# A two-layer decoder step on one core: both feed-forward up projections as one level of Strassen's scheme, with their results passing through DRAM

## The reference

```
def rmsnorm(x, g):
    xf = x.astype(jnp.float32)
    y = xf * lax.rsqrt(jnp.mean(xf * xf, axis=-1, keepdims=True) + EPS)
    return (y * g.astype(jnp.float32)).astype(x.dtype)

def sq_relu_mlp(x, w_up, w_down):
    h = jax.nn.relu(x @ w_up)
    return (h * h) @ w_down
...
        h = h + mix.astype(h.dtype)
        h = h + sq_relu_mlp(rmsnorm(h, p["norm_mlp"][layer]), p["w_up"][layer], p["w_down"][layer])
```

## Time and profile before

| | us |
|---|---|
| median of 3 runs | 2968.97 |
| lowest and highest of the runs | 2967.33, 2970.69 |
| span of the profiled execution | 2965.2 |
| PE busy in it | 2851.3 (96%) |
| DVE, ACT, POOL busy | 1339.4, 517.6, 721.5 |

### The profile page before, as it was taken

One profiled execution on the slowest core, in us unless ns is written; L12 is line 12 of the kernel. 1 busy time (PEld: TensorE's weight loads), 2 busy tenths in 40 slices (PEclk: granted clock), 3 DMA queues, 4 the chain that ended last, 5 costly groups with the idle time before them and its releaser, 6 DMA issues. The chain is left out here.

```text
span 2965.2 us, 51232 instructions
## 1 busy us (share of the span) xinstructions
PE 2851.3 (96%) x21758; PEld 2709.3 (91%) x21758; DVE 1339.4 (45%) x1746; ACT 517.6 (17%) x827; POOL 721.5 (24%) x437
## 2 busy tenths in 40 slices
PE   6999999999999999999998999899999999999997
PEld 6989898889999999999988898766899999999997
DVE  6665555646422332323546666355454223332233
ACT  3222222212000000000213444333210000000001
POOL 2100000013333333333321110112233333333331
PEclk8999999999999999999999999999999999999998
DMA  4111111211111111111211001466111111111111
GB/s 110 52 53 53 53 53 53 93 33 50 44 49 45 43 50 44 43 50 43 55 38 28 30 28 34 178 262 246 41 44 43 44 50 43 49 45 43 47 47 72
DMA packets 211773, 183.92 MB, mean 62 GB/s; under 512 B 21777, under 2 KB 199745, under 8 KB 209505
## 3 DMA queue, kind: packets, MB, share of 16 engines
q1 hardware_dynamic: 176192, 123.58, 13.8%
...
## 5 line engine op out<-in xcount | busy, mean ns | idle before, releaser
L156 POOL CAST w_hi<-w_raw 128x1024 fp32r<-128x1024 f32 (+2 forms) x148 | 143.0, 967 | 1194.7 <-PEq L1227 975.7
L158 POOL TENSOR_TENSOR w_lo<-w_raw,w_hi 128x1024 fp32r<-128x1024 f32 (+2 forms) x148 | 396.7, 2681 | 11.9
L1425 DVE TENSOR_TENSOR h<-h,G 128x1050 f32<-128x1050 f32 x120 | 149.7, 1247 | 482.6 <-PE G L217 482.6
L217 PE MATMUL G<-a_lo,w_hi 128*128 128x350 f32 x1536 | 330.8, 323 | 0.0
L217 PE MATMUL G<-a_hi,w_hi 128*128 128x350 f32 x1536 | 330.6, 323 | 0.0
L217 PE MATMUL G<-a_hi,w_lo 128*128 128x350 f32 x1536 | 330.2, 323 | 0.0
L1356 ACT ACTIVATE a_hi<-ua 128x1050 fp32r<-128x1050 f32 x64 | 69.4, 1084 | 1219.9 <-DVE ua L1415 1219.9
L217 PEld LDWEIGHTS G<-a_lo,w_hi 128*128 128x128 f32 x1536 | 262.7, 189 | 0.0
L1412 DVE TENSOR_TENSOR ua<-G,rstd 128x1050 f32<-128x1050 f32 x64 | 80.1, 1252 | 402.3 <-PE G L217 402.2
L217 PEld LDWEIGHTS G<-a_hi,w_hi 128*128 128x128 f32 x1536 | 261.5, 189 | 0.0
L217 PEld LDWEIGHTS G<-a_hi,w_lo 128*128 128x128 f32 x1536 | 260.9, 189 | 0.0
...
## 6 DMA issues: line engine op xcount, KB each, us to landing
w_raw<-in_w_up SPq DMA_DIRECT2D x64, 512.0 KB, 4.2
w_raw<-in_w_down SPq DMA_DIRECT2D x64, 512.0 KB, 3.4
w_raw<-in_hg_wq SPq DMA_DIRECT2D x8, 512.0 KB, 3.8
w_raw<-in_hg_wf SPq DMA_DIRECT2D x8, 512.0 KB, 3.8
w_raw<-in_hg_wi SPq DMA_DIRECT2D x8, 512.0 KB, 3.9
w_raw<-in_hg_wg SPq DMA_DIRECT2D x8, 512.0 KB, 4.2
s_old<-in_state_hgrn ACTq DMA_DIRECT2D x8, 512.0 KB, 5.5
out_state_hgrn_sample<-s_new ACTq DMA_DIRECT2D x8, 512.0 KB, 3.7
```

What stands on the lines that cost most here:

```text
L156: nc.gpsimd.tensor_copy(high, raw).then_inc(k.w_hi_done, 1)
L158: nc.gpsimd.tensor_tensor(low, raw, high, ALU.subtract).then_inc(k.w_split, 1)
L217: last = nc.tensor.matmul(out, w(a, t), x(b, t, c), start=(t == 0 and (a, b) == ORDER[0]), stop=(t == nk - 1 and (a, b) == ORDER[-1]))
L1425: nc.vector.tensor_tensor(h, h, tile(k, (g0 + 1 + t) % 2), ALU.add).then_inc(k.g_free, 1)
```

## The change

Per layer, the up projection W^T X is cut into 2 x 2 quarters. W^T (4096 hidden features x 1024) is cut along the model's features into those of even and of odd tiles of h, and along the hidden features into even and odd blocks of 128; the 1048 tokens are cut into two halves of 524. A pair p (of 16) is two blocks of hidden features, with weight quarters A11, A12, A21, A22 of 128 x 512 numbers; the activations' quarters B11, B21, B22 and their sums T1 to T4 are made once. Per pair PE makes 7 products of half the depth and half the tokens in place of 8: a product is 4 x 3 x 2 = 24 matmuls of 262 columns. These are Strassen's scheme in the form with 15 additions: DVE makes four sums of weights S1 to S4 per pair, ACT all seven high parts, POOL all seven low parts, and the sums of products are mostly made by accumulation in PSUM, with a copy of an intermediate state (E1, E2, E3 by ACT) before the accumulation goes on, which DVE adds later. Each quarter of the result, 128 x 524, gets relu and `rstd` by DVE (`scale`), the square by ACT, and is stored to DRAM (`kept_a`).

The up projection of all hidden features now comes first, then the down projection in 8 groups, whose activations are loaded again from DRAM and split into high (ACT) and low parts (DVE). While the up projection runs, 7 of the 8 tiles of h are in DRAM (`kept_h`), and odd pairs' weights use their room. The down projection's matmuls, weight loads and splits are as before. Semaphores of the recurrent layer are given back so that there are enough for `Mlp`.

```diff
-W_GROUP, G_GROUP = 8, 12
+W_GROUP, G_GROUP = 4, 8
+HALF = PROMPT // 2 + DEC // 2
+QUARTER = HALF // 2
+PAIRS = D_FF // (2 * P)
+KH = KD // 2
...
+OPERANDS = {"P1": ("A11", "B11"), "P2": ("A12", "B21"), "P3": ("S4", "B22"), "P4": ("A22", "T4"),
+            "P5": ("S1", "T1"), "P6": ("S2", "T2"), "P7": ("S3", "T3")}
+WEIGHTS = ("A11", "A12", "S2", "S1", "S3", "A22", "S4")
...
     def pool(self, pool):
+        for p in range(PAIRS):
+            for x in WEIGHTS:
+                pool.wait_ge(self.w_high, self.at("w_high", WEIGHT[x, p]))
+                pool.wait_ge(self.summed, self.at("summed", SUM["S3" if x == "A11" else "S4", p]))
+                nc.gpsimd.tensor_tensor(self.w_lo[p % 2][x][:, :, :], self.w_raw[p % 2][x][:, :, :],
+                                        self.w_hi[p % 2][x][:, :, :], ALU.subtract).then_inc(self.w_ready, 1)
         split_blocks(k, pool, W_GROUP * GROUPS, n0=self.w0)
...
+        def product(x, p, slot, first=False):
+            a, b = OPERANDS[x]
+            pe.wait_ge(self.w_ready, self.at("w_ready", WEIGHT[a, p]))
...
+            for j in range(KH):
+                if p == 0:
+                    pe.wait_ge(self.x_low, self.at("x_low", LOW_X[b, j]))
+                for u, v in ORDER:
+                    for c in range(2):
+                        last = nc.tensor.matmul(self.bank(slot, c), w[u][:, j, :],
+                                                moving[v][:, j, c * QUARTER:(c + 1) * QUARTER],
...
+        product("P1", 0, "a0", True)
+        product("P2", 0, "b", True)
+        pe.wait_ge(k.g_free, g0)
+        norm()
+        for i in range(PAIRS):
+            if i > 0:
...
+                product("P1", i, f"a{i % 2}", True)
+                pe.wait_ge(self.early_out, self.at("early_out", EARLY_OUT["E3", i - 1]))
+                product("P4", i - 1, f"a{(i - 1) % 2}")
+                pe.wait_ge(self.taken, self.at("taken", TAKEN["C11", i - 1]))
+                product("P2", i, "b", True)
+                pe.wait_ge(self.taken, self.at("taken", TAKEN["C22", i - 1]))
+                product("P3", i - 1, "c")
+            pe.wait_ge(self.early_out, self.at("early_out", EARLY_OUT["E1", i]))
+            product("P6", i, f"a{i % 2}")
+            if i > 0:
+                pe.wait_ge(self.taken, self.at("taken", TAKEN["C12", i - 1]))
...
+            product("P5", i, "c", True)
+            pe.wait_ge(self.early_out, self.at("early_out", EARLY_OUT["E2", i]))
+            product("P7", i, f"a{i % 2}")
...
+        dve.wait_ge(self.squared, self.at("squared", QUARTERS["C12", last]))
+        for j in range(RINGS):
+            dve.wait_ge(self.a_stored[j], self.at("a_stored", 16 * (4 * PAIRS // RINGS)))
+        clear(1)
+        clear(2)
+        for t in range(KD):
+            if t < KD - 1:
+                dve.wait_ge(self.h_back[t], self.at("h_back", 16))
+            add(g0, t)
```

More of the change, by code:

```diff
@@ new lines, with counted, in_steps @@
+SUMS = ("S1", "S2", "S3", "S4")
+FIRST_X, LATER_X = ("B11", "B21", "T2", "T1"), ("T3", "T4", "B22")
+LAST_WEIGHT_AT = ("A11", "A12", "S2", "S1", "S3", "A22", "S4")
+def counted(*events):
+    return {e: n + 1 for n, e in enumerate(events)}
+def in_steps(early, late, middle=(), last=()):
+    out = []
+    for i in range(PAIRS + 1):
+        out += [(e, i - 1) for e in early if i > 0]
+        out += [(e, i) for e in middle if i < PAIRS]
+        out += [(e, i - 1) for e in late if i > 0]
+        out += [(e, i) for e in last if i < PAIRS]
+    return out
@@ new lines, in product_order @@
+def product_order():
+    out = []
+    for i in range(PAIRS + 1):
+        for e, lag in (("P1", 0), ("P4", 1), ("P2", 0), ("P3", 1), ("P6", 0), ("P5", 0), ("P7", 0)):
+            if 0 <= i - lag < PAIRS:
+                out.append((e, i - lag))
+    return out
+PRODUCT = counted(*product_order())
+EARLY_OUT = counted(*in_steps(("E3",), (), ("E1",), ("E2",)))
+QUARTERS = counted(*in_steps(("C22", "C21"), ("C12",), ("C11",)))
+TAKEN = counted(*[e for e in QUARTERS if e[0] != "C21"])
+WEIGHT = counted(*[(x, p) for p in range(PAIRS) for x in WEIGHTS])
@@ new lines, in norm @@
+        def norm():
+            pe.wait_ge(self.sq_summed, self.at("sq_summed", SQUARE[KD - 1, 1]))
+            for n in range(4):
+                last = nc.tensor.matmul(self.bank("a1" if n >= 2 else "c", n % 2), k.ones[:, :],
+                                        k.rstd[:, n * QUARTER:(n + 1) * QUARTER], start=True, stop=True)
+            last.then_inc(self.norm_done, 1)
+        pe.wait_ge(k.g_free, g0 - 1)
+        for b in range(2):
+            pe.wait_ge(k.m_free[b], k.m_read[b])
@@ new lines, in pe @@
+        pe.wait_ge(k.w_split, w0 + 3)
+        pe.wait_ge(self.quarter, self.at("quarter", QUARTERS["C21", last]))
+        for n, col in enumerate((0, P)):
+            if n:
+                pe.wait_ge(self.taken, self.at("taken", TAKEN["C12", last]))
+            for t in range(GROUP):
+                if n == 0:
+                    pe.wait_ge(self.a_ready, self.at("a_ready", t + 1))
+                ins = products(nc, banks(k, (g0 + n) % 2), w_parts(k, 0, 2 * P, col), moving(0), (t,), GROUP)
+            ins.then_inc(k.g_done, 1)
@@ L1394, in pe @@
[L1394 removed]
+                group(i * 2 + 1 + half, 1 + half)
+        group(GROUPS - 1, 1)
         if self.latent_next:
@@ new lines, in dve @@
+        dve.wait_ge(k.dve_apart, self.layer + 1)
+        for j in range(KH):
+            dve.wait_ge(self.x_exact, self.at("x_exact", EXACT_X["T4a", j]))
+            raw = self.op_raw["T4"][:, j, :]
+            nc.vector.scalar_tensor_tensor(out=raw, in0=self.side(2 * j, 0), scalar=k.g_back[:, 2 * j:2 * j + 1],
+                                           in1=raw, op0=ALU.mult, op1=ALU.add).then_inc(self.x_exact, 1)
+        for j in range(KH):
+            self.low_x(dve, "T3", j)
+        dve.wait_ge(self.rooted, self.at("rooted", 2))
@@ new lines, in dve, with add, group @@
+        last = PAIRS - 1
+        clear(0)
+        for j in range(GROUP):
+            low_a(0, j, 0)
+        take("C22", last)
+        take("C21", last)
+        take("C12", last)
+        def add(g, t):
+            dve.wait_ge(k.g_done, g + t + 1)
+            h = in3(k.h[:, t, :])
+            nc.vector.tensor_tensor(h, h, tile(k, (g0 + t) % 2), ALU.add).then_inc(k.g_free, 1)
+        def group(g, buffer):
+            for t in range(KH):
+                add(g_at(g), t)
+            for j in range(GROUP):
+                low_a(g + 1, j, buffer)
+            for t in range(KH, KD):
+                add(g_at(g), t)
@@ L1444, in dve @@
         else:
-            take_down(g_last)
+            for t in range(KD):
+                add(g_last, t)
 class Keys:
```

613 lines of the change are left out of this document (481 added, 132 removed).

## The result

The changed kernel takes 2922.4 us (median of 4 runs, 2921.6 to 2924.6) against 2969.5 for the kernel before: a ratio of 0.9848, 95% interval 0.9834 to 0.9862, faster by 47 us. Measured again beside later experiments it was 2921.5 against 2967.0. The prediction was 2931, with a range of 2908 to 2964. The profiled execution has a span of 2922.8 us, against 2965.2 before.

What follows compares the result with a forecast made beforehand. PE's matmul starts were taken to bound the feed-forward parts. Savings of 42.2 us per layer, less start costs, plus 5 per layer of old start overhead, gave -23.5 and -14.1, together -37.6 us: span 2927.6, median 2931, range 2908 to 2964.

Steps and rivals of the forecast that it cites:

- The pitch: Up projection: 262-column matmuls start 122.5 ns apart on PE, 329.3 us per layer, saving 42.2 us per layer.
- rival E: Up projection: weight loads set the pace, 141 ns per 262-column matmul, ending at 3030 us; chance 0.04.
- Within a pair: Up-projection pair of 20.6 us on PE: DVE's 7, ACT's 8.5 and POOL's 9 us stay hidden, no stall.
- Rival D: Each up-projection pair: PE waits once if A22's load lands more than 2.1 us later; 2994 us, chance 0.14.
- The start: Start of each feed-forward part: 34.7 us of chain less 14.7 of useful work, PE loses 20.0 us per layer.
- hold-offs by POOL: Start of a feed-forward part: about six POOL subtractions hold DVE off, some 1.1 us each, 6.6 us.
- Half the clock: Behind the idle at a feed-forward part's start, PE runs at 1.2 GHz, costing 2.7 us once per layer.
- Layer 0's extra wait: Layer 0, before pair 0's first product: PE waits 11 us (8 to 15) for DVE's queue, then POOL.
- The down projection's start: Start of the down projection: 8.3 MB cross in 25 us at 332 GB/s, no wait; 1 us per layer counted.
- rival C: Down projection's start: mixed loads and stores run nearer 200 GB/s, +12 us per layer, 2955 us; chance 0.14.
- The down projection has the same matmuls: nothing: Down projection: matmuls are unchanged, so nothing is saved there; tiles taken at 5.77 us each.
- A: Whole kernel: the forecast as worked out holds, 2915 to 2947 us, likeliest 2931; chance 0.55.

Runs made afterwards that it cites:

- E3: Not a run: ACT's copy of an intermediate state of a sum of products in PSUM, before the accumulation goes on; DVE adds it later.

## Why the prediction was right, point by point

**The pitch** was taken as 122.5 ns and is 122.0 in layer 0 and 122.3 in layer 1; 2688 matmuls cost 327.8 and 328.7 us in place of 329.3. The old tiles' 371.5 us are near too: from start to start of the 2304 matmuls of the kernel before it was 372.4 and 371.3. So 44.6 and 42.6 us were saved where 42.2 were forecast. Choosing the 256-column row as the nearest was right for a reason that the prediction didn't have: 128 columns lie on the floor and 256 beyond it, so the straight line between 128 and 350 of rival E had no meaning. The rule of the Trainium skill, "TensorE: Matmul & The Clock Gate", section "Back-to-back issue gap", gives about 81 ns at 128 columns and 131 at 512 in a stream of loads and matmuls. The trace agrees with neither end: 111.7 ns at 128, and 161 ns already at 350. The measured distances decide here.

**Within a pair** no wait was forecast, and there is none. The work of the other engines is hidden as said: in 240 us DVE is busy for 96.5, ACT for 93.9, POOL for 104.8, so 8.2, 8.0 and 8.9 us of a pair against the forecast's 7, 8.5 and 9. Rival D put the slack at 2.1 us and the price beyond it at the wait itself; the runs gave a slack of 2.6, and a price of 111 us for 89 us of waits, a quarter more, by the lost overlap and the clock.

**The start** is where the forecast was right in sum by luck: two errors nearly cancel. From the last add to P1 of pair 1, 34.7 us were forecast; layer 1 has 2206.88 - 2173.43 = 33.5 and layer 0 35.3. Of these the chain up to S3 was given 32.8 us, with 6.6 of hold-offs by POOL, and took 29.0 in layer 1: the same instructions without hold-offs were given 26.2, so that what is left for hold-offs is some 2.8 us. In layer 1 the four instructions of T3 (from 2178.65 on) and the first four of T4 (from 2182.38 on) take 3.81 and 3.88 us, each four beside one subtraction of POOL; the latter take 2.78 in layer 0, from 738.38 on, where POOL is idle. So a hold-off did cost about 1.1 us, but only two of the six that were counted are seen; two of POOL's later subtractions fell beside the reciprocal, which kept its 6.69 us. The step "P1 of pair 1 needs the low part of A11, which POOL makes only after DVE's S3" left out ACT, which added 2.6 us; moving its square away showed it. The rest, POOL's 1.8 us, was as forecast. Against the useful work of 14.7 us PE lost 33.1 - 14.6 = 18.4 us in layer 1 where 20.0 was said, 14.0 of them the one wait. Half the clock cost 2.1 us where 2.7 was said (20 matmuls in 4.49 us in place of 2.44).

**Layer 0's extra wait** was forecast at 11 us and is 10.5. Two tiles took DVE 7.83 us where 7.7 was said:

```profile
698.38 0.75 DVE L1823 SCALAR_TENSOR_TENSOR T_raw<-h,g_mlp,T_raw 128x524 f32<-128x524 f32 x1
...
714.05 0.76 DVE L1823 SCALAR_TENSOR_TENSOR T_raw<-h,g_mlp,T_raw 128x524 f32<-128x524 f32 x1
```

(15.67 us for four tiles.) The clock fell to a half behind this wait too, so that layer 0 paid for it twice, which the prediction counted once:

```profile
728.00:733.40 5.40, 5.40 (x25) 5.40 (x26) 5.40 (x6) 4.37 (x8) 2.68 (x2) 0.50 0.00 0
```

**The down projection's start**: 8.3 MB in 25 us and no wait were forecast. No wait came. The transfers reached 350 GB/s over 25 us, loads and stores mixed, and DVE's first add started at 1085.5, just behind the last store. PE's third tile needs it done at 1078.5 + 11.6 = 1090.1. It ended at 1086.8, so rival C was 3.3 us away, and its reason, that a mix of both directions would be slower, is refuted here:

```profile
1060.00:1085.00 25.00, 24.30 (x187) 24.09 (x186) 11.14 (x15) 8.30 (x11) 7.84 (x4) 1.00 0.98 350
```

```profile
1085.39 0.07 DVE L1933 MEMSET a_hi<- 128x8 f32 x1 [5.07 <-DMA kept_a<-ring]
...
1085.54 1.25 DVE L1953 TENSOR_TENSOR h<-h,G 128x1050 f32<-128x1050 f32 x1
```

The 1 us counted there was a wait of 0.7 for E3 before P4 of the last pair.

**"The down projection has the same matmuls: nothing"** holds within about 2 us per layer, but the 5.77 us per tile of the earlier trace rows are from one of its cheapest groups. In the kernel before DVE's adds of a group lie 5.77 or 5.79 us apart in layer 0, by turns, and 5.80 or 5.84 in layer 1, as here:

```profile
2389.08 1.25 DVE L1425 TENSOR_TENSOR h<-h,G 128x1050 f32<-128x1050 f32 x1 [4.59 <-PE G L217]
2394.92 1.25 DVE L1425 TENSOR_TENSOR h<-h,G 128x1050 f32<-128x1050 f32 x1 [4.59 <-PE G L217]
```

In the changed kernel two adds 50 tiles apart are:

```profile
1113.64 1.25 DVE L1953 TENSOR_TENSOR h<-h,G 128x1050 f32<-128x1050 f32 x1 [2.36 <-PE G L234]
...
1403.72 1.25 DVE L1953 TENSOR_TENSOR h<-h,G 128x1050 f32<-128x1050 f32 x1 [4.56 <-PE G L234]
```

That is 290.08 / 50 = 5.80 us per tile. From start to start, the 2304 down matmuls of a layer took 371.0 and 373.1 us before and take 371.4 and 370.9 now: 0.4 more in layer 0, 2.2 less in layer 1. Why equal matmuls lie 160.3 to 162.2 ns apart from group to group stays open. Since the prediction took its tile of 5.77 for all 64, it also put what the old parts had beyond their tiles too high: 7.1 and 8.4 us, where the matmuls' starts leave 4.5 and 4.7. Of these it counted 5, which was nearly right.

**The sum**, layer 1: -42.6 of the up projection, +21.9 at the starts (16.3 idle, 1.6 of the norm's product, 2.1 of clock, 0.7 at the last P4, and 1.2 of restarts and remainders), -2.2 of the down tiles, -4.7 of what stood beside the old tiles: -27.6 where -23.5 was said. Layer 0: -44.6 + 33.4 + 0.4 - 4.5 = -15.3 where -14.1 was said. The starts' last items are what is left, not measured by themselves. The likeliest case, A, held, at its lower side: the sum was off by 5.3 us, of which the up projections gave 2.8, the down projections 1.8 and layer 1's start 1.5, while layer 0's start took 0.8 back. The forecast median was 8.6 us too high, since it also carried over that the median stood 3.8 us above the span; here it is 0.4 below the span of the execution that was profiled (2924.6 us).
